# Down projection as seven half-size block products on one Trainium2 core: token-major output, block sums of `a` on GpSimd

## The reference

```python
def swiglu(h, w_gate, w_up, w_down):
    return (jax.nn.silu(h @ w_gate) * (h @ w_up)) @ w_down
...
        h = rmsnorm(x, g_norm2[l]) * (1.0 + sc2) + sh2
        x = x + gt2 * swiglu(h, w_gate[l], w_up[l], w_down[l])
    return rmsnorm(x, g_final)
```

## Time and profile before

| | |
|---|---|
| median of 3 runs | 2304.01 us (2303.28 to 2304.23) |
| span of the profiled execution | 2303.3 us (the profile gives no other time of that execution; its span is 0.7 us under the median) |
| mean granted TensorE clock | 0.987 of full speed |
| busy: TensorE, VectorE, ScalarE, GpSimd | 2249.0, 1532.3, 887.8, 233.0 us |
| a gate and up unit | 78.0 us |
| first product of the down projection | 1803.3 us |
| last product of the down projection | starts 2291.6, next instruction 2291.7, taken as ended at 2291.9 us |
| products in it | 2016 of 512 columns, 192 of 256 |
| bytes moved, mean rate | 404 MB, 176 GB/s |

### The profile page before, as it was taken

The page is one execution under the profiler, slowest core; times in us unless marked ns, Lnnn a source line. Parts: engine busy times, 40 slices in busy tenths (PEclk is TensorE's granted clock), DMA queues, the critical chain, the costliest instruction groups (busy, mean ns, idle before and its releaser), DMA issues.

```text
span 2303.3 us, 27075 instructions
## 1 busy us (share of the span) xinstructions
PE 2249.0 (98%) x10486; PEld 1866.6 (81%) x10486; DVE 1532.3 (67%) x1734; ACT 887.8 (39%) x1048; POOL 233.0 (10%) x90
## 2 busy tenths in 40 slices
PE   5999999999999999999999999999999999999998
PEld 5878878888877788788888888888888888888887
DVE  5968667474766757677887788778878544444444
ACT  4333232323246222444444444444444433333333
POOL 0002433333420013000000000000000001010001
PEclk7999999999999999999999999999999999999999
DMA  9943444444541777234444445344434845554553
GB/s 362 377 143 114 166 145 148 150 163 161 183 166 37 275 266 263 92 102 146 155 164 137 145 138 173 128 138 163 160 131 148 326 184 203 193 188 183 192 193 128
DMA packets 188198, 404.43 MB, mean 176 GB/s; under 512 B 11328, under 2 KB 67920, under 8 KB 172496
## 3 DMA queue, kind: packets, MB, share of 16 engines
q1 hardware_dynamic: 175088, 387.10, 47.4%
q10 hardware_dynamic: 13024, 16.13, 2.0%
HBM read 383.27 MB, written 19.92 MB: 175 GB/s over the span
## 4 chain that ended last, share of the span: by engine, by line
PE 90%; DVE 4%; issue 2%; ACT 1%; DMA 1%; POOL 1%; SPq 1%; POOLq 0%; DVEq 0%; ACTq 0%
PE ps L1791 27%; PE ps L1793 27%; PE ps L1792 27%; PE ps L1948 1%; DVE acc L1102 1%; DMA araw<-in_w_ada 1%; PE ps L2235 1%; PE ps L1961 1%; PE ps L1959 1%; DVE acc L1339 1%; PE ps L1882 0%; PE ps L1823 0%; PE ps L2060 0%; PE ps L1937 0%; PE ps L1843 0%
## 5 line engine op out<-in xcount | busy, mean ns | idle before, releaser
L931 ACT ACTIVATE whi<-wraw 128x1024 fp32r<-128x1024 f32 x200 | 211.0, 1061 | 276.5 <-DVE wraw L1614 153.3
L1595 DVE TENSOR_TENSOR wlo<-wraw,whi 128x1024 fp32r<-128x1024 f32 x200 | 240.6, 1219 | 76.8 <-ACT whi L931 76.8
L1791 PE MATMUL ps<-d_hi,whi 128*128 128x512 f32 (+1 forms) x736 | 280.1, 381 | 0.0
L1793 PE MATMUL ps<-d_hi,wlo 128*128 128x512 f32 (+1 forms) x736 | 279.6, 380 | 0.0
L1792 PE MATMUL ps<-d_lo,whi 128*128 128x512 f32 (+1 forms) x736 | 279.6, 380 | 0.0
L1791 PE MATMUL ps<-h_hi,whi 128*128 128x512 f32 x680 | 271.6, 399 | 0.0
L1793 PE MATMUL ps<-h_hi,wlo 128*128 128x512 f32 x680 | 267.0, 393 | 0.0
L1792 PE MATMUL ps<-h_lo,whi 128*128 128x512 f32 x680 | 266.5, 392 | 0.0
L1707 DVE TENSOR_TENSOR d_lo<-d_raw,d_hi 128x2048 fp32r<-128x2048 f32 (+1 forms) x44 | 99.7, 2267 | 243.3 <-ACT d_hi L998 243.3
L1791 PE MATMUL ps<-whi,sk_hi 128*128 128x512 f32 x640 | 250.8, 392 | 0.0
L1793 PE MATMUL ps<-whi,sk_lo 128*128 128x512 f32 x640 | 249.4, 390 | 0.0
(11 more groups left out here) (332 smaller groups left out, 3866.3 us busy)
## 6 DMA issues: line engine op xcount, KB each, us to landing
araw<-in_w_ada SPq DMA_DIRECT2D x64, 1024.0 KB, 6.0
wraw<-in_w_gate SPq DMA_DIRECT2D x88, 512.0 KB, 3.9
wraw<-in_w_up SPq DMA_DIRECT2D x88, 512.0 KB, 4.7
d_raw<-aT_keep SPq DMA_DIRECT2D x44, 1024.0 KB, 4.8
wraw<-in_w_down SPq DMA_DIRECT2D x44, 1024.0 KB, 7.1
wraw<-in_w_in SPq DMA_DIRECT2D x38, 1024.0 KB, 5.3
...
```

The lines of the kernel that those rows point to most:

```text
L931: A(EHI[e % 4], src, ACT.Copy).then_inc(uhi_ok, 1)
L1595: V_.tensor_tensor(ELO[e % 4], src, EHI[e % 4].bitcast(F32), ALU.subtract).then_inc(ulo_ok, 1)
L1791: pe.matmul(o, w_hi, m_hi, start=first, stop=False)
L1793: return pe.matmul(o, w_lo, m_hi, start=False, stop=last)
```

## The change

The down projection becomes a 2 x 2 block product as well. A chunk of `a` is cut into two halves of its channels and two of the tokens, the weights into two halves of the chunk's rows and pairs of 512 output columns ("near" and "far"); output columns are done in two halves of 1024 (n). For each chunk there are seven products: P1, P5, P6, P4 in an "early" step and P7, P2, P3 in a "late" one, 44 steps in the order n, early or late, chunk. An entry is one product of a step: 12 matmuls with a block of `a` stationary and 512 weight columns moving, so the output is token-major. `DOWN` lists the 154 entries.

- The sums of `a`'s blocks are made once: in each unit GpSimd forms three of them and an intermediate (`combine_a`, four operations of 512 elements per partition), ScalarE stores the seven blocks in `a_keep` (`turned`, `keep_sums`: five DMAs a unit where there were two).
- SyncE loads four blocks of `a` and four pieces of weights of 0.5 MB for an early step, three and three for a late one, still two steps deep; a load of weights waits for the last low part of the step two before.
- ScalarE makes the high parts entry by entry (`down_hi`) and those of the blocks (`block_hi`); VectorE makes the low parts of the weights (`down_lo`, 1024 elements) and their block sums (`down_sum`: three in an early step, one in a late one).
- The low parts of `a`'s blocks move from VectorE to GpSimd (`block_lo`, two operations a step).
- VectorE combines the products (`mix_p6`, `mix_p5`, `mix_p4`, `take`), scales three of the sums (`pre_scale`) and adds them to x1 (`pre_add`). x1 is turned to token-major in PSUM banks 6 and 7 in late steps of the first half of the columns (`turn_x1`, 64 transposes). For the first half of the columns the last joins to x1 and the multiplication by the final gain are GpSimd's (`join_x1`, `gain`, eight operations of 1024 elements in the second half's early steps); for the second half VectorE joins.
- The sums of squares are ScalarE's alone (`x2_squares`, with accumulator). Scaling and output of all four token blocks stand after the last join.

```diff
+        def down_order(s):
+
+            n, late, j = down_step(s)
+            if late:
+                if s < STEPS - 2:
+                    return [(s, "P7"), (s, "P2"), (s, "P3")]
+                return [(s + i, p) for ps_ in (("P7", "P2"), ("P3",)) for i in range(2) for p in ps_] if s == STEPS - 2 else []
+            if s == 0:
+                return [(0, "P1"), (0, "P5"), (0, "P6")]
+            if s == 1:
+                return [(1, "P1"), (1, "P5"), (0, "P4"), (1, "P6"), (1, "P4")]
+            return [(s, p) for p in (("P1", "P6", "P5", "P4") if j == NCH - 1 else ("P1", "P5", "P6", "P4"))]
+
+        DOWN = [x for s in range(STEPS) for x in down_order(s)]
+        def sums_after(e):
+
+            due = [(s, name, FIRST_E[s] + i - 2 + (s == 2) + (s == STEPS - 1))
+                   for s in range(STEPS) for i, name in enumerate(("P7",) if down_step(s)[1] else ("P5", "P6", "P4"))]
+            return [(s, name) for s, name, at_e in due if max(at_e, -1) == e]
...
+            def down_loads(s):
+
+                n, late, j = down_step(s)
+                lower, upper = slice(j * S, j * S + HT), slice(j * S + HT, j * S + S)
+                near, far = slice(2 * n * S, 2 * n * S + S), slice(2 * n * S + S, 2 * n * S + 2 * S)
+                if s < 2:
+                    sp.wait_ge(ulo_ok, 28 * NU - 3 + 3 * s)
+                else:
+                    sp.wait_ge(ulo_ok, E0 + END_E[s - 2])
+                for i, (rows, col) in enumerate(((lower, far), (upper, far), (upper, near)) if late else
+                                                ((lower, near), (lower, far), (upper, far), (upper, near))):
+                    sp.dma_start(DRAW[s % 2][i].rearrange("p (k c) -> p k c", k=2),
+                                 w_down[0, rows, col].rearrange("(k p) c -> p k c", p=P)).then_inc(dw_ld[s % 2][i], 16)
+
...
+            def combine_a(u):
+
+                pool.wait_ge(tr_sb, 4 * u)
+                if not (isinstance(u, int) and u == 1):
+                    pool.wait_ge(as_st, 32 * u - 32)
+                a11, a12, a21, a22 = (stT[h][:, 2 * q:2 * q + 2, :] for h in range(2) for q in range(2))
+                s2, s3 = (sA[:, i, :].rearrange("p (k t) -> p k t", k=2) for i in range(2))
+                s4 = sB[:].rearrange("p (k t) -> p k t", k=2)
+                pool.tensor_tensor(s3, a11, a21, ALU.subtract).then_inc(ac_ok, 1)
+                pool.wait_ge(ac_ok, 4 * u - 3)
+                pool.tensor_tensor(a21, a21, a22, ALU.subtract).then_inc(ac_ok, 1)
+                pool.wait_ge(ac_ok, 4 * u - 2)
+                pool.tensor_tensor(s2, a21, a11, ALU.subtract).then_inc(ac_ok, 1)
+                pool.wait_ge(ac_ok, 4 * u - 1)
+                pool.tensor_tensor(s4, a12, s2, ALU.add).then_inc(ac_ok, 1)
+
...
+            def block_lo(s):
+
+                late = down_step(s)[1]
+                for i, part in enumerate((slice(0, 2), slice(2, 3 if late else 4))):
+                    pool.wait_ge(dah_ok, 2 * s + i + 1)
+                    pool.tensor_tensor(d_lo[s % 2][:, part, :], d_raw[s % 2][:, part, :],
+                                       d_hi[s % 2][:, part, :].bitcast(F32), ALU.subtract).then_inc(dal_ok, 1)
+
+            def join_x1(n, i):
+
+                pool.wait_ge(t_ok, 4 * n + i + 1)
+                h, c, t, op = ((1, 0, tmp[0], ALU.add), (1, 1, tmp[1], ALU.subtract),
+                               (0, 0, kept, ALU.add), (0, 1, left, ALU.add))[i]
+                part = x2[:, 2 * h:2 * h + 2, (2 * n + c) * S:(2 * n + c + 1) * S]
+                pool.tensor_tensor(part, part, t[:], op).then_inc(x2_ok, 1)
+
...
+            def gain(n, i):
+
+                h, c = ((1, 0), (1, 1), (0, 0), (0, 1))[i]
+                pool.wait_ge(ssq_ok, TB + 8 * n + 2 * i + 2)
+                if n == 0 and i == 0:
+                    pool.wait_ge(x_ld[0], 16 + 16)
+                cols_ = slice((2 * n + c) * S, (2 * n + c + 1) * S)
+                part = x2[:, 2 * h:2 * h + 2, cols_]
+                pool.tensor_tensor(part, part, gfb[:, cols_].unsqueeze(1).to_broadcast([P, 2, S]), ALU.mult)\
+                    .then_inc(z_ok, 1)
+
+            block_lo(0)
+            block_lo(1)
+            combine_a(NCH)
+            for s in range(2, STEPS):
+                block_lo(s)
+                if 2 * NCH <= s < 2 * NCH + 4:
+                    join_x1(0, s - 2 * NCH)
+                elif 2 * NCH + 4 <= s < 2 * NCH + 8:
+                    gain(0, s - 2 * NCH - 4)
+
+            def final_rs(h):
+                pool.wait_ge(n_ms, 1 + h + 1)
+                two = slice(2 - 2 * h, 4 - 2 * h)
+                pool.tensor_tensor(rs[:, two], ve[:, two], halfneg[:, two], ALU.pow).then_inc(n_rs, 1)
+
+            gain(1, 0)
+            gain(1, 1)
+            final_rs(0)
+            gain(1, 2)
+            final_rs(1)
...
+            def keep_sums(u, rows):
+
+                act.wait_ge(ac_ok, 4 * u)
+                act.dma_start(a_keep[rows, 1, :], stT[1][:, 0:2, :].rearrange("p k t -> p (k t)")).then_inc(at_st[1], 16)
+                act.dma_start(a_keep[rows, 2:5:2, :], sA[:]).then_inc(as_st, 16)
+                act.dma_start(a_keep[rows, 6, :], sB[:]).then_inc(as_st, 16)
...
+            def block_hi(s):
+
+                late = down_step(s)[1]
+                act.wait_ge(da_ld[s % 2], 16 * (s // 2 + 1))
+                if s < 2:
+                    act.wait_ge(u_used, 28 * NU - 9 + 3 * s)
...
+                    act.wait_ge(u_used, E0 + END_E[s - 2])
+                for part in (slice(0, 2), slice(2, 3 if late else 4)):
+                    A(d_hi[s % 2][:, part, :], d_raw[s % 2][:, part, :], ACT.Copy).then_inc(dah_ok, 1)
...
-            def down_lo(d):
-
-                dve.wait_ge(dhi_ok, 2 * d + 1)
-                last = d == 4 * NCH - 1
-                tokens = slice(0, HT if last else S)
-                V_.tensor_tensor(d_lo[d % 2][:, :, tokens], d_raw[d % 2][:, :, tokens],
-                                 d_hi[d % 2][:, :, tokens].bitcast(F32), ALU.subtract).then_inc(dlo_ok, 1)
-                if d == 0:
+            def down_lo(e):
+
+                s, name = DOWN[e]
+                dve.wait_ge(uhi_ok, E0 + e + 1)
+                V_.tensor_tensor(ELO[e % 4], DRAW[s % 2][D_RAW[name]], EHI[e % 4].bitcast(F32), ALU.subtract)\
+                    .then_inc(ulo_ok, 1)
+
+            def down_sum(s, name):
+
+                i = {"P5": 1, "P6": 2, "P4": 3, "P7": 0}[name]
+                for k in ((0, 1) if name in ("P5", "P7") else (i,)):
+                    dve.wait_ge(dw_ld[s % 2][k], d_loads(s, k))
+                if name in ("P6", "P4"):
+                    dve.wait_ge(usum_ok, d_sums(s, name) - 1)
+                other = DRAW[s % 2][1 if name == "P7" else i - 1]
+                V_.tensor_tensor(DRAW[s % 2][i], DRAW[s % 2][i], other, ALU.add).then_inc(usum_ok, 1)
+
...
+            def join_x1(i, b=None):
+
+                h, c, t, op = ((1, 0, tmp[0], ALU.add), (1, 1, tmp[1], ALU.subtract),
+                               (0, 0, kept, ALU.add), (0, 1, left, ALU.add))[i]
+                dve.wait_ge(t_ok, 4 + i + 1 + (b or 0))
+                if b is None:
+                    V_.tensor_tensor(x2_part(1, h, c), x2_part(1, h, c), t[:], op).then_inc(x2_ok, 1)
+                else:
+                    part = x2[:, 2 * h + b, (2 + c) * S:(3 + c) * S]
+                    V_.tensor_tensor(part, part, t[:, b, :], op).then_inc(x2_ok, 1)
+
+            def final_mean(h):
+
+                two = slice(2 - 2 * h, 4 - 2 * h)
+                dve.wait_ge(ssq_ok, TB + 12 + 4 * h)
+                ch.link(V_.reduce_sum(ssq[:, two], ssq4[:, two, :], axis=AX.X))
+                V_.tensor_scalar(ve[:, two], ssq[:, two], 1.0 / D, EPS, ALU.mult, ALU.add).then_inc(n_ms, 1)
+
+            def scaled_out(h):
+
+                tb = 2 - 2 * h
+                dve.wait_ge(n_rs, 1 + h + 1)
+                dve.wait_ge(z_ok, 6 + h)
+                if h:
+                    dve.wait_ge(mix_ok, 13)
+                V_.tensor_scalar(x2[:, tb, :], x2[:, tb, :], rs[:, tb:tb + 1], None, ALU.mult).then_inc(y_ok[0], 1)
+
...
+            take(1, 0)
+            join_x1(0)
+            take(1, 1)
+            join_x1(1)
+            take(1, 2)
+            join_x1(2)
+            final_mean(0)
+            for b in range(2):
+                dve.wait_ge(u_used, E0 + end_of(1, "P3") + b)
+                take(1, 3, b)
+                join_x1(3, b)
+            final_mean(1)
+            dve.wait_ge(ssq_ok, TB + 16)
+            V_.tensor_tensor(x2_part(1, 0, 1), x2_part(1, 0, 1), both(gfb[:, 3 * S:4 * S]), ALU.mult).then_inc(mix_ok, 1)
+            scaled_out(0)
+            scaled_out(1)
...
+            def down_entry(e):
+
+                s, name = DOWN[e]
+                n, late, j = down_step(s)
+                blk, bank = D_BLK[name], DBANK[n][name]
+                pe.wait_ge(dal_ok, 2 * s + blk // 2 + 1)
+                pe.wait_ge(ulo_ok, E0 + e + 1)
...
```

(10 more changed lines are left out.)

510 lines of the change are left out of this document (290 added, 220 removed).

## The result

The changed kernel takes **2355.92 us** (median of 4 runs, 2353.3 to 2358.9) beside 2304.12 us before (4 runs of the same session, 2303.28 to 2306.12): 1.0222 times as long, 95% interval 1.0208 to 1.0236. The forecast was 2313 us with a range up to 2338. Its direction holds and its size does not: 52 us slower instead of 9.

A forecast was written before the change was run, and what follows sets the result against it. VectorE and GpSimd, excluding each other, were to replace TensorE as bound in early down-projection steps. Down projection 490.2 us (+1.6) and tail +7.9 on 2303.3 gave a 2312.8 us span, forecast 2313; range 2285 to 2338.

The forecast's parts named there:

- TensorE alone, 427.6 us: Down projection: TensorE's own products and transposes need 427.6 us, 61.2 less, if nothing else were slower.
- The exclusion and its price: Down projection: a GpSimd operation excludes VectorE's with two SBUF inputs, costing 2.13 us per 1024 elements; early step 12.24 us.
- 33.8 from the terms: Second half's early steps over TensorE's time: two-engine excess, GpSimd joins and gains +17.0, VectorE PSUM operations +4.8, less lead.
- The units: Gate and up units: GpSimd's four sums fit into VectorE's waits, cost nothing, and units stay at 78.0 us.
- TensorE stays the bound: Rival, down projection: under 1.45 us per GpSimd operation, early steps keep TensorE's pace; 2251 us or somewhat more; 15%.
- The tail: After the last product: 7.3 us of operations, then output of 4.19 MB; 19.3 us instead of 11.4, +7.9.
- the account of the late steps: Late steps, 7.72 against 8.16 us: spare time absorbs 11.6 us of VectorE work in the first half; +6.8 in the second.
- +10.1: Start of down projection: GpSimd's four sums of a and ten VectorE operations from PSUM, hidden before, add 10.1 us.
- slower still: the loads: Rival, down projection: late weights and blocks of a lengthen 22 to 44 steps by 1 us; 2335 to 2357 us; 12%.
- against it: Evidence against the late-loads rival: from 1936 us on, the DMA engines' share is half.
- 10 us for waits in which both engines stand behind each other: Allowance in the forecast's upper bound for VectorE and GpSimd waiting in order; with no lead, 2330 us.

The follow-up runs named there:

- e4: Changed kernel with GpSimd's low parts cut to 4 of 512 columns from step 2 on and a's blocks loaded ahead of the weights; 2277.9 us.
- e5: Changed kernel with three extra 1 MB loads (final gains, x1's first two pieces) issued at steps 5, 7 and 9 instead of 2; 2347.4 us.
- e11: Changed kernel with the second half's seven gains and sums of mixed products spread one to a late step; 2356.8 us.
- e3: Changed kernel with GpSimd's low parts of a's blocks cut to 4 of 512 columns from step 2 on; 2288.1 us.
- e2: Changed kernel with the load of a's blocks issued ahead of the step's weights instead of behind them; 2345.4 us.

## Why the prediction was right in its sign and wrong in its size

**Right.**
- *TensorE alone, 427.6 us.* With the low parts narrow and the blocks loaded first (e4), three of the four phases take 97.7, 123.1 and 89.7 us against 96.8, 119.7 and 89.8; the first early phase, with the unchanged start in it, takes 134.5 against 121.4.
- *The exclusion and its price.* 2.20 us per operation against 2.13 assumed; the early step 12.36 against 12.24 (e5). The early phase of the second half came out at 36.2 us over TensorE's time against 33.8 from the terms. This closeness is in part luck: the phase took 5.2 us more in e11 without an edit in it, and step 22 alone took 20.8 us.
- *The units.* 78.0 us, with GpSimd's sums in place.
- *The sign.* The rival "TensorE stays the bound" needed under 1.45 us an operation, and it is 2.20.
- *The tail.* 21.7 us against 19.3. The four outputs are issued together at 2345.3 to 2348.4. Two of its terms came from no row: the square with its accumulator, 0.8, measured 0.63 and 0.19, and the mean, 0.5, measured 0.16 and 0.17 where nothing stood in the way. Missing was that even a small operation can wait: the mean's last step on two elements lasts 2.12 us instead of 0.17, behind a gain on GpSimd.

**Wrong**, 44 us of span (2357.1 against 2312.8). The table has it as 23.1 in the late phases, 9.8 at the start, 6.5 and 2.4 in the early ones and 2.4 in the tail. The mechanism was right. The step that failed is the account of the late steps: work put into them was priced at nothing in the first half of the columns and at 6.8 us in the second, because their spare time was added up. A start without delay and loads without a price come behind it:
1. *The late steps, 23 us of it.* The term "in the first half the spare 11 x 0.44 + 7.0 = 11.8 takes them; in the second +6.8" added up what eleven steps have to spare as one account. They measured 12.3 and 17.6 us over TensorE's time. e3 shows that this too is GpSimd's low parts: without them 97.2 and 89.7. A step whose sum is 7.72 us did not run at 8.16 but at 8.8 to 9.2 (33 to 35), and one with a pair of gains and sums at 10.27 (37 and 38), where its sum is 10.0. Four late steps of the first half (12 to 14 and 16) did run at 9.1, which with their transposes is TensorE's own time. So a step's sum was a lower bound. Why it is passed by 0.6 to 1 us is not shown by a run of its own; the trace has the operations in an order, in which GpSimd's pair of 4.7 us waits for ScalarE, and its first operation has to be done before the step's first products, its second before P3's.
2. *The start, 9.8 us, of which 6.3 belong to it and 3.5 to the execution ahead of the stage.* "+10.1" was laid on VectorE's account for the phase, with the first product left at 1803.3. The first product came 6.1 us after TensorE was free. It waits for a bank, which VectorE's mg (L1847) frees, and mg stands behind the whole queue. VectorE's timeline: four operations over 13 us, each behind one of GpSimd's four.

```profile
1798.29 3.44 DVE L1944 TENSOR_TENSOR wraw<-wraw 128x1024 f32<-128x1024 f32 x1
1801.83 3.25 DVE L1944 TENSOR_TENSOR acc<-acc,wraw 128x1024 f32<-128x1024 f32 x1
1805.00 3.40 DVE L1933 TENSOR_TENSOR wlo<-wraw,whi 128x1024 fp32r<-128x1024 f32 x1
1808.33 3.35 DVE L1944 TENSOR_TENSOR araw<-araw,acc 128x1024 f32<-128x1024 f32 x1
...
1798.14 12.46 POOL L693 TENSOR_TENSOR d_lo<-d_raw,d_hi 128x1024 fp32r<-128x1024 f32 x4 [35.59 <-ACT d_hi L1165]
...
1813.03 0.76 PE L2101 MATMUL ps<-whi,d_hi 128*128 128x512 f32 x1 [6.14 <-DVE mg L1847]
```

3. *The loads, 6.5 us by the table.* The rival "slower still: the loads" got 12% and was to be seen as 22 to 44 steps of 1 us. It came in small and in few places. The extra loads (e5) cost 6.3 us in step 2. The order (e2) leaves step 2 at 19.1 us and takes 2.3 us off step 1, 3.7 off step 3 and 2.4 off step 6; the whole stage is 7.0 us shorter. Its "against it" looked at the share of the DMA engines from 1936 on, half in the earlier trace rows; in the changed kernel the first late phase has 0.80 and step 2 all of it. What was missing is that the extra 3.1 MB were not put in the queue at all.
4. *The bound "10 us for waits in which both engines stand behind each other".* It was to cover all of this, and it came from no row. The measured span is 44 us over the sum, and the time is 26 us over the bound of 2330.

One thing that makes waits dearer was left out. TensorE's granted clock was 1.00 through the stage before; in the changed kernel it is at 0.5, the lower of its two levels (1.2 GHz), for 43.6 us of the stage, behind waits. The rows above have a mean of 0.95 for the first early phase and 0.94 for the second, against 1.00 in the earlier trace rows. By the distance of starts in TensorE's timeline the stage has some 44 gaps, 68 us in all, and 80 to 90 products at the lower level, each some 0.2 us longer, 16 to 18 us together; e4 has 6 gaps, 12.2 us, and some 20 such products, 4 us. This is contained in the phases above and comes on top of the waits ahead of it. No run takes it away by itself.
